# A decoder trunk's recurrence in another order: the first turned blocks later, the solve at the end of its own group, the masks ahead of the sample's steps, and the group norm centred by one product

## The chip, the cores and the metric

The kernel runs on one core of one Trainium2 chip. The metric is the device time of one execution in microseconds. The kernel before took 1679.8 us (median of 3 runs, 1679.66 to 1681.52).

## The reference

Two layers of a hybrid decoder act on a prompt of 256 tokens and on eight single sample tokens (264 columns in all, model width 1024). Each layer is a SwiGLU block, a mixer and a second SwiGLU block. The mixer's RWKV-7 group has 16 heads of 64; for each token it does

```
Sa = einsum('bhij,bhj->bhi', S, -kk_t)
S = S * w_t[:, :, None, :] + Sa[..., None] * b_t[:, :, None, :] + v_t[..., None] * k_t[:, :, None, :]
y_t = einsum('bhij,bhj->bhi', S, r_t)
...
mean = jnp.mean(y, axis=-1, keepdims=True)
var = jnp.mean(jnp.square(y - mean), axis=-1, keepdims=True)
y = ((y - mean) * lax.rsqrt(var + RWKV_GN_EPS)).reshape(Bsz, L, RWKV_DIM)
y = y * ln_w.astype(f32) + ln_b.astype(f32)
```

A short convolution group and a Mamba-2 group stand beside it; the three outputs are concatenated and multiplied by `w_out`.

## The kernel before

Each layer has a front stage (projections) and a back stage (`back_stage`), and only the back stage is touched. The five engines have one instruction list each, written out by hand. They meet by semaphores, and each list is done strictly in order, so the order of the calls is the schedule.

The 16 heads are worked as 8 pairs (`RT = 8`), one pair on 128 partitions. The prompt's recurrence is done in chunks of 64 tokens (`C = 64`, `NCH = 4`). Within a chunk the triangular system is inverted by doubling, in five levels (`LV = 5`), and several pairs are in the works at once. Loop turn `g` starts pair `g`, continues pair `b = g - 1`, does the states and outputs of pair `c = g - 2`, and the group norm of pair `p = g - 3`; `g` runs from 0 to 9. What the steps are, by their names:

- TensorE: `turn` transposes tokens, `gram(g+1)` makes the products of the next pair, `turn_x` puts the start of the inverse into PSUM, `level_t1(p, i)` and `level_u(p, i)` are the two products of a level (16 small matmuls each), `gv` and `solve` make u and w, `transfer`, `own_outputs`, `own_states` and `chunk` carry the state over the chunks, `turn_final` turns the last state, `mean_of` and `variance_of` sum over the 64 channels of each head, and `short(n)` are 24 large matmuls of the output projection with the two other groups' part (in turns 8 and 9, where pairs run out).
- ACT copies results from PSUM: `t1_copy` between the two products of a level, `x_copy` after a level, `tokens`, `rv_copy`, `uw_copy`, `state_copy`, `y_copy`, `variance`, and it squares (`square`). In turn 8 it also computes the inverse roots of five pairs' variances (`Ln`, then `Exp`, each with a load of its table), and it makes the high halves of weights (`ws.split_hi`).
- DVE: `mask` (two per pair, L2026), `start` (adds the identity, L2032), `turn_blocks` (L2038), `finish` (L2042), `transfer` (L2049, L2051), the eight steps `step(b, 0..7)` of the sample tokens (L2063 to L2081), `centre` (L2086), `gated` (L2092), scalings, and `ws.split_lo`.
- POOL: the first level (L1772), `level(p, i)` (the masked products of a level, two buffers, L1750), `weigh(g+1)` (four instructions, L1744), `key_row(b)` (L1758), `short_split_lo` (L1764), `ws.split_lo` (L216).

For pair `b` a level goes: `level` (POOL), `level_t1` (PE), `t1_copy` (ACT), `level_u` (PE, which also needs the blocks turned by DVE's `turn_blocks`), `x_copy` (ACT). `order_of` numbers the levels over all pairs, and `copied` the copies. PSUM bank `WB` is shared in turn by `gv`, `solve`, `mean_of` and `variance_of`. A new pair begins with `gram`, two masks, POOL's first level, `start`, and `turn_x`.

## Time and profile before

| | |
|---|---|
| median of 3 runs | 1679.8 us |
| the profiled execution | 1676.1 us, its span 1674.1 us |
| TensorE busy | 1550.2 us, 93% |
| VectorE busy | 1108.9 us, 66% |
| ScalarE busy | 881.6 us, 53% |
| GpSimd busy | 271.7 us, 16% |
| TensorE's mean granted clock | 0.978 |

The span goes from the first to the last instruction of one profiled execution. Times in rows are microseconds from its start. A timeline row has the start, the duration, the engine, the line, the operation, output and inputs with their shapes, the count of merged instructions, and in brackets the idle time before it with what ended it. TensorE's matmuls overlap, so the distance between two starts tells what a block of them takes to issue, and the duration how long until its last result is there. The back stages lie at about 440 to 605 us (layer 0) and 1266 to 1430 us (layer 1). The granted clock is 1.0 for TensorE's upper level of 2.4 GHz and 0.5 for the lower of 1.2 GHz.

### The profile page before, as it was taken

Reading aid. Unit: us, or ns where it says so; the run is one execution under the profiler, and the core shown is the slowest. Engines: PE = TensorE matmul, PEld = TensorE weight load, DVE = VectorE, ACT = ScalarE, POOL = GpSimd, SP = SyncE. Lnnn points to the kernel's source line nnn. Section 1 sums busy time; section 2 is a strip of 40 time slices with the busy share of each in tenths; the row PEclk is TensorE's granted clock in tenths of the full one; section 3 lists DMA queues with packets and bytes.
Section 4 is the critical chain, followed back from the end, with each engine's and each line's share of the span. In section 5 each row is a group of like instructions: output and inputs, shape, how many; then the busy total and the mean of one; then the engine's idle time right before and its main releaser. Section 6 shows DMA issues by size and latency. Waiting matters only on the chain. (4 is left out here: it accounts for less than half of the span.)

```text
span 1674.1 us, 39220 instructions
## 1 busy us (share of the span) xinstructions
PE 1550.2 (93%) x16355; PEld 1463.3 (87%) x16355; DVE 1108.9 (66%) x1758; ACT 881.6 (53%) x1579; POOL 271.7 (16%) x259
## 2 busy tenths in 40 slices
PE   7999999999688889999999999999996898899997
PEld 6999999987577789999999999989775777899997
DVE  5565587785577757665475655968765777576654
ACT  5444464767355655444353444647673456554443
POOL 0000003001265621000000000030013665300000
PEclk9999999999889999999999999999997999999999
DMA  7555556371134545655454655643702446355552
GB/s 229 178 177 165 168 170 203 112 209 50 50 106 130 156 135 176 193 162 188 163 185 151 202 165 177 192 151 117 224 1 72 122 132 183 118 185 193 178 181 71
DMA packets 280642, 256.15 MB, mean 153 GB/s; under 512 B 48054, under 2 KB 268700, under 8 KB 280450
## 3 DMA queue, kind: packets, MB, share of 16 engines
q1 hardware_dynamic: 276698, 252.05, 48.7%
q8 instruction: 131, 2.15, 0.6%
q10 hardware_dynamic: 3768, 1.59, 0.4%
q14 instruction: 45, 0.37, 0.1%
HBM read 242.22 MB, written 11.38 MB: 151 GB/s over the span
## 5 line engine op out<-in xcount | busy, mean ns | idle before, releaser
L209 ACT ACTIVATE front_hi<-front_raw 128x1024 fp32r<-128x1024 f32 (+2 forms) x230 | 238.5, 1039 | 260.7 <-PE ps L234 249.5
L216 DVE TENSOR_TENSOR front_lo<-front_raw,front_hi 128x1024 fp32r<-128x1024 f32 (+1 forms) x210 | 252.3, 1201 | 109.4 <-ACT front_hi L209 108.4
L209 ACT ACTIVATE out_hi<-out_raw 128x1024 fp32r<-128x1024 f32 (+1 forms) x168 | 173.2, 1038 | 215.6 <-PE ps L234 201.3
L216 DVE TENSOR_TENSOR out_lo<-out_raw,out_hi 128x1024 fp32r<-128x1024 f32 (+1 forms) x148 | 179.7, 1214 | 106.2 <-ACT out_hi L209 105.4
L232 PE MATMUL ps<-front_h_hi,front_hi 128*128 128x264 f32 (+1 forms) x816 | 240.8, 295 | 4.9 <-DVE front_lo L216 3.3
L234 PE MATMUL ps<-front_h_hi,front_lo 128*128 128x264 f32 (+1 forms) x816 | 232.4, 285 | 0.0
L233 PE MATMUL ps<-front_h_lo,front_hi 128*128 128x264 f32 (+1 forms) x816 | 232.3, 285 | 0.0
L232 PE MATMUL ps<-ffn_h_hi,out_hi 128*128 128x264 f32 x704 | 200.4, 285 | 0.1
L233 PE MATMUL ps<-ffn_h_lo,out_hi 128*128 128x264 f32 x704 | 199.6, 284 | 0.0
L234 PE MATMUL ps<-ffn_h_hi,out_lo 128*128 128x264 f32 x704 | 199.6, 283 | 0.0
L232 PE MATMUL ps<-in_h_hi,front_hi 128*128 128x264 f32 x688 | 196.5, 286 | 0.0
L233 PE MATMUL ps<-in_h_lo,front_hi 128*128 128x264 f32 x688 | 195.6, 284 | 0.0
L234 PE MATMUL ps<-in_h_hi,front_lo 128*128 128x264 f32 x688 | 195.6, 284 | 0.0
L232 PEld LDWEIGHTS ps<-front_h_hi,front_hi 128*128 128x128 f32 (+1 forms) x816 | 153.7, 188 | 13.6 <-issue 11.9
L233 PEld LDWEIGHTS ps<-front_h_lo,front_hi 128*128 128x128 f32 (+1 forms) x816 | 153.7, 188 | 0.7
L234 PEld LDWEIGHTS ps<-front_h_hi,front_lo 128*128 128x128 f32 (+1 forms) x816 | 153.0, 188 | 0.1
L216 POOL TENSOR_TENSOR front_lo<-front_raw,front_hi 128x1024 fp32r<-128x1024 f32 (+1 forms) x20 | 49.8, 2490 | 543.0 <-ACT front_hi L209 543.0
L232 PEld LDWEIGHTS ps<-ffn_h_hi,out_hi 128*128 128x128 f32 x704 | 132.4, 188 | 0.6 <-ACT ffn_h_hi L283 0.5
L233 PEld LDWEIGHTS ps<-ffn_h_lo,out_hi 128*128 128x128 f32 x704 | 132.4, 188 | 0.1
L234 PEld LDWEIGHTS ps<-ffn_h_hi,out_lo 128*128 128x128 f32 x704 | 132.3, 188 | 0.0
L233 PEld LDWEIGHTS ps<-in_h_lo,front_hi 128*128 128x128 f32 x688 | 130.4, 190 | 0.1
L232 PEld LDWEIGHTS ps<-in_h_hi,front_hi 128*128 128x128 f32 x688 | 130.3, 189 | 0.1
(400 smaller groups left out, 3826.2 us busy)
## 6 DMA issues: line engine op xcount, KB each, us to landing
front_raw<-in_w_in SPq DMA_DIRECT2D x50, 1024.0 KB, 5.3
out_raw<-in_ffn_w_in SPq DMA_DIRECT2D x44, 1024.0 KB, 5.2
front_raw<-in_ffn_w_in SPq DMA_DIRECT2D x40, 1024.0 KB, 5.3
back_sample_rows<-row_scratch SPq DMA_DIRECT2D x160, 128.0 KB, 3.1
out_raw<-in_w_out SPq DMA_DIRECT2D x16, 1024.0 KB, 5.2
front_raw<-in_ffn_w_out SPq DMA_DIRECT2D x16, 896.0 KB, 4.7
out_raw<-in_ffn_w_out SPq DMA_DIRECT2D x16, 896.0 KB, 4.7
front_raw<-in_ffn_w_out SPq DMA_DIRECT2D x8, 1024.0 KB, 5.0
```

The lines of the kernel that those rows point to most:

```text
L209: act.activation(self.hi[n % self.RING][:, 0:k, 0:w], self._raw(n), ACT.Copy).then_inc(self.hi_ready, 1)
L216: eng.tensor_tensor(self.lo[n % self.RING][:, 0:k, 0:w], self._raw(n), self.hi[n % self.RING][:, 0:k, 0:w].bitcast(F32), ALU.subtract).the ...
L232: pe.matmul(out, hi[:, j, 0:w], x_hi[:, j], start=start and j == 0, stop=False)
L233: pe.matmul(out, hi[:, j, 0:w], x_lo[:, j], start=False, stop=False)
L234: mm = pe.matmul(out, lo[:, j, 0:w], x_hi[:, j], start=False, stop=stop and j == k - 1)
```

## The change

Nothing of the recurrence's arithmetic is added or left out; most of the diff moves calls.

- **TensorE.** `solve` moves from the head of the next turn (`solve(c)`) to the end of its own (`solve(b)`). The token transposes `turn(g, 0)` and `turn(g, 1)` go together ahead of `level_u(b, 2)`, and `turn_x(g)` behind it. The order of levels becomes (b, 2), (b, 3), (g, 0), (b, 4), (g, 1), where it was (b, 2), (g, 0), (b, 3), (g, 1), (b, 4). `variance_of(p)` goes behind `gram(g+1)`. In turn 8 `short(0)` stands between `level_t1(7, 2)` and `level_u(7, 2)`; in turn 9 `short(2)` stands behind `transfer(7)`.
- **DVE.** `turn_blocks(b, 2)` moves from the end of the group that made them (`turn_blocks(g, 2)`) to the head of the next. The masks of the next pair are ahead of steps 4 and 5. `transfer(c)` is ahead of `turn_blocks(b, 3)`. The scalings of `ys` are spread over four turns, two in each.
- **POOL.** `weigh(g+1)` is ahead of `level(g, 0)`, `level(b, 2)` is at the head of the next turn (in turn 8 behind `short_split_lo` and `ws.split_lo`).
- **ACT.** Follows TensorE's order; `decays` run one pair further ahead; `variance(p)` is directly ahead of `t1_copy(b, 4)`.
- **Group norm.** A new constant `centre` is the identity less 1/64 in each head's block. `mean_of` multiplies by it and so gives the deviation itself, in PSUM. DVE's `centre` goes; `square` and `gated` read PSUM, `gated` waits for `square`, and `variance_of`, which writes the same bank, waits for `gated`.

```diff
+    parts["centre"] = np.eye(P) - same / HS
...
-            order = [(g - 1, 2), (g, 0), (g - 1, 3), (g, 1), (g - 1, 4)]
+            order = [(g - 1, 2), (g - 1, 3), (g, 0), (g - 1, 4), (g, 1)]
...
-            for pair, i in [(g, 0), (g - 1, 3), (g, 1), (g - 1, 4), (g, 2)]:
+            for pair, i in [(g - 1, 3), (g, 0), (g - 1, 4), (g, 1), (g, 2)]:
```

GpSimd's list:

```diff
-                        level(g, 0)
                     if b >= 0:
+                        level(b, 2)
                         level(b, 3)
                     if g + 1 < RT:
                         weigh(g + 1)
                     if g < RT:
-                        level(g, 1)
-                    if g == RT - 1:
-                        for q in range(3):
-                            short_split_lo(q)
+                        level(g, 0)
                     if b >= 0:
                         level(b, 4)
                     if g == RT:
                         ws.split_lo(pool, 2)
+                    if g < RT:
+                        level(g, 1)
                     if b >= 0:
                         key_row(b)
                     if g == RT - 1:
-                        short_split_lo(3)
-                    if g < RT:
-                        level(g, 2)
-                    if g == RT - 1:
+                        for q in range(4):
+                            short_split_lo(q)
                         ws.split_lo(pool, 0)
```

The group norm:

```diff
-                    act.wait_ge(s("dev_done"), p + 1)
+                    act.wait_ge(s("mean_ps"), p + 1)
...
-                    act.activation(v[:, p], dev[:, p], ACT.Square).then_inc(s("dev_sq"), 1)
+                    act.activation(v[:, p], ps[:, WB, 0:N], ACT.Square).then_inc(s("dev_sq"), 1)
...
-                def centre(p):
-                    dve.wait_ge(s("mean_ps"), p + 1)
-                    dve.scalar_tensor_tensor(out=dev[:, p], in0=ps[:, WB, 0:N], scalar=-1.0 / HS, in1=r[:, p],
-                                             op0=ALU.mult, op1=ALU.add).then_inc(s("dev_done"), 1)
...
-                    dve.wait_ge(s("dev_done"), p + 1)
+                    dve.wait_ge(s("dev_sq"), p + 1)
...
-                    pe.matmul(ps[:, WB, 0:N], head, r[:, p], start=True, stop=True).then_inc(s("mean_ps"), 1)
+                    pe.matmul(ps[:, WB, 0:N], centre, r[:, p], start=True, stop=True).then_inc(s("mean_ps"), 1)
...
+                    pe.wait_ge(s("dev_gated"), p + 1)
```

TensorE's turn after the change, as its calls follow (conditions left out):

```
level_t1(b, 2); turn_final(c - 1); turn(g, 0); turn(g, 1); short(0) in turn 8; level_u(b, 2); turn_x(g)
transfer(c); short(2) in turn 9; level_t1(b, 3); mean_of(p); level_u(b, 3); level_t1(g, 0); short(3) in turn 9
own_outputs(c); own_states(c); level_u(g, 0); level_t1(b, 4); chunk(c, 1); short(1) in turn 8; gram(g + 1)
variance_of(p); level_u(b, 4); level_t1(g, 1); chunk(c, 2); gv(b); level_u(g, 1); chunk(c, 3); solve(b)
```

ACT's turn after the change:

```
uw_copy(c); t1_copy(b, 2); split_hi(4), split_hi(5) in turn 9; final_copy(c - 1); tokens(g, 0); tokens(g, 1)
x_copy(b, 3); x_copy(g, 0); Ln, Exp, split_hi(2) in turn 8; t1_copy(b, 3); square(p); x_copy(b, 4)
t1_copy(g, 0); state_copy(c, 0); x_copy(g, 1); decays(g + 2); variance(p); t1_copy(b, 4); state_copy(c, 1)
split_hi(3) in turn 8; t1_copy(g, 1); rv_copy(b); state_copy(c, 2); x_copy(g, 2); state_copy(c, 3); y_copy(c)
split_hi(0), split_hi(1) in turn 7; two y copies in turn 8
```

## Rows read from the trace of the kernel before

**Rows 1.** The page, busy time, share and instructions of each engine.
```profile
PE 1550.2 (93%) x16355; PEld 1463.3 (87%) x16355; DVE 1108.9 (66%) x1758; ACT 881.6 (53%) x1579; POOL 271.7 (16%) x259
```
**Rows 2.** Waits, 440 to 600 us: us in total, times, longest.
```profile
PE ps L2230 <- DVE back_inverse_t L2032: 10.8, 8, 3.6
PE ps L2275 <- DVE back_inverse_t L2042: 5.5, 5, 3.8
```
**Rows 3.** Timeline of TensorE in the middle of layer 0's back stage.
```profile
523.94 0.68 PE L2230 MATMUL ps<-cst,back_inverse_t 64*64 64x64 f32 x16 [1.03 <-DVE back_inverse_t L2032]
...
536.57 1.09 PE L2275 MATMUL ps<-back_gv_a,back_inverse_t 64*64 64x128 f32 x16 [0.29 <-DVE back_inverse_t L2042]
...
538.91 0.68 PE L2230 MATMUL ps<-cst,back_inverse_t 64*64 64x64 f32 x16 [1.02 <-DVE back_inverse_t L2032]
539.43 0.63 PE L2218 MATMUL ps<-back_n_x,back_inverse_t 64*64 64x64 f32 x16
```
**Rows 4.** Timeline of TensorE: `turn_x(1)`, and `level_u` of pairs 0 and 6, both layers.
```profile
458.12 1.12 PE L2230 MATMUL ps<-cst,back_inverse_t 64*64 64x64 f32 x16 [3.61 <-DVE back_inverse_t L2032]
459.02 1.06 PE L2218 MATMUL ps<-back_n_x,back_inverse_t 64*64 64x64 f32 x16
...
554.99 0.63 PE L2218 MATMUL ps<-back_n_x,back_inverse_t 64*64 64x64 f32 x16
...
1285.13 1.06 PE L2218 MATMUL ps<-back_n_x,back_inverse_t 64*64 64x64 f32 x16
...
1378.80 0.63 PE L2218 MATMUL ps<-back_n_x,back_inverse_t 64*64 64x64 f32 x16
```
**Rows 5.** Timeline of ACT: the copy of a variance in a middle group.
```profile
532.06 0.39 ACT L1873 ACTIVATE xs<-ps 128x264 f32<-128x264 f32 x1 [0.30 <-PE ps L2355]
```
**Rows 6.** Timeline of DVE in two middle groups.
```profile
532.34 0.95 DVE L2092 SCALAR_TENSOR_TENSOR gate<-xs,cols,gate 128x264 f32<-128x264 f32 x1
...
534.29 1.29 DVE L2026 TENSOR_TENSOR back_products<-ps,cst 128x512 f32<-128x512 f32 x2
...
544.67 0.42 DVE L2086 SCALAR_TENSOR_TENSOR xs<-ps,xs 128x264 f32<-128x264 f32 x1
```
**Rows 7.** Timeline of POOL in turn 7 of layer 0.
```profile
559.88 4.73 POOL L1764 TENSOR_TENSOR short_lo<-y_short,short_hi 128x528 fp32r<-128x528 f32 x3 [2.18 <-ACT short_hi L1863]
...
569.98 2.58 POOL L216 TENSOR_TENSOR out_lo<-out_raw,out_hi 128x1024 fp32r<-128x1024 f32 x1 [1.11 <-ACT out_hi L209]
```
**Rows 8.** Timeline of ACT in turns 8 and 9 of layer 0.
```profile
572.88 0.39 ACT L1829 ACTIVATE back_inverse<-ps 128x256 f32<-128x256 f32 x1 [1.14 <-PE ps L2218]
...
579.45 0.36 ACT L1822 ACTIVATE back_n_x<-ps 128x256 f32<-128x256 f32 x1
...
591.04 1.99 ACT L209 ACTIVATE out_hi<-out_raw 128x1024 fp32r<-128x1024 f32 x2
```
**Rows 9.** Timeline of TensorE in turns 8 and 9 of layer 0, `mean_of(6)` also of layer 1.
```profile
572.17 0.68 PE L2218 MATMUL ps<-back_n_x,back_inverse_t 64*64 64x64 f32 x15 [0.73 <-issue]
...
575.90 0.46 PE L2296 MATMUL ps<-back_tok,back_u_w 64*64 64x64 f32 x16
...
579.87 0.62 PE L2218 MATMUL ps<-back_n_x,back_inverse_t 64*64 64x64 f32 x13 [1.56 <-ACT back_n_x L1822]
...
593.34 0.46 PE L2296 MATMUL ps<-back_tok,back_u_w 64*64 64x64 f32 x16 [1.79 <-ACT back_final_state L1854]
...
593.97 0.71 PE L2351 MATMUL ps<-xs,cst 128*128 128x264 f32 x2
...
1417.51 0.71 PE L2351 MATMUL ps<-xs,cst 128*128 128x264 f32 x2
```
**Rows 10.** Windows: stretch, length, busy time of engines, granted clock, DMA share, GB/s.
```profile
458.00:463.00 5.00, 4.88 (x72) 4.44 (x74) 1.08 (x3) 2.25 (x6) 2.43 (x4) 0.50 0.03 3
...
842.00:846.00 4.00, 2.85 (x13) 2.88 (x14) 1.23 (x1) 2.87 (x3) 0.75 (x5) 0.59 0.41 116
```
**Rows 11.** Timeline of TensorE between the layers.
```profile
843.15 0.56 PE L232 MATMUL ps<-in_h_hi,first_hi 128*128 128x264 f32 x1 [3.39 <-PEq L143]
```

More of the change, by code:

```diff
@@ L1907, in _ @@
                         decays(1)
+                    if c >= 0:
+                        uw_copy(c)
                     if 0 <= b < RT:
@@ L1929, in _ @@
                         ws.split_hi(act, 2)
+                    if 0 <= b < RT:
+                        t1_copy(b, 3)
+                    if p >= 0:
+                        square(p)
+                    if 0 <= b < RT:
+                        x_copy(b, 4)
+                    if g == RT - 1:
+                        short_split_hi(0)
+                        short_split_hi(1)
                     if g < RT:
@@ L1940, in _ @@
                         shift_store(3 * g)
-                        if g == 1:
-                            shift_rows(4)
-                    if g == RT - 1:
-                        short_split_hi(0)
-                        short_split_hi(1)
-                    if 0 <= b < RT:
-                        t1_copy(b, 3)
-                    if g < RT:
-                        tokens(g, 1)
-                    if p >= 0:
-                        square(p)
-                    if 0 <= b < RT:
-                        x_copy(b, 4)
+                    if g + 2 < RT:
+                        decays(g + 2)
+                    if p >= 0:
+                        variance(p)
+                    if 0 <= b < RT:
+                        t1_copy(b, 4)
+                    if c >= 0:
+                        state_copy(c, 1)
+                    if g == 1:
+                        shift_rows(5)
+                        shift_store(4)
                     if g == RT - 1:
@@ L2113, in _ @@
                     if 0 <= b < RT:
+                        step(b, 0)
+                    if c >= 0:
+                        transfer(c)
+                    if 0 <= b < RT:
                         turn_blocks(b, 3)
-                        step(b, 0)
+                        step(b, 1)
                     if g == RT + 1:
                         ws.split_lo(dve, 3)
-                    if c >= 0:
-                        transfer(c)
+                    if p >= 0:
+                        gated(p)
+                    if 0 <= b < RT:
+                        turn_blocks(b, 4)
+                        step(b, 2)
                     if g < RT:
@@ L2122, in _ @@
                     if 0 <= b < RT:
-                        step(b, 1)
-                    if p >= 0:
-                        centre(p)
+                        step(b, 3)
+                    if g + 1 < RT:
+                        mask(g + 1, 0)
+                        mask(g + 1, 1)
                     if 0 <= b < RT:
-                        step(b, 2)
-                        turn_blocks(b, 4)
-                        step(b, 3)
-                    if p >= 0:
-                        gated(p)
-                    if g < RT:
-                        turn_blocks(g, 2)
+                        step(b, 4)
+                        step(b, 5)
+                        finish(b)
                     if g < 4:
@@ L2162, in _ @@
                 y_split_lo(1)
-                centre(RT - 1)
                 gated(RT - 1)
@@ L2394, in _ @@
                         shift_turn(4)
-                    if c >= 0:
-                        solve(c)
                     if c >= 1:
                         turn_final(c - 1)
-                    if g == RT + 1:
-                        short(2)
-                    if g < RT:
-                        turn_x(g)
+                    if g and g < RT:
+                        turn(g, 0)
+                        turn(g, 1)
+                    if g == RT:
+                        short(0)
                     if 0 <= b < RT:
@@ L2405, in _ @@
                     if g < RT:
-                        level_t1(g, 0)
-                        turn(g, 0)
-                    if g == RT:
-                        short(0)
+                        turn_x(g)
                     if c >= 0:
                         transfer(c)
+                    if g == RT + 1:
+                        short(2)
+                    if 0 <= b < RT:
+                        level_t1(b, 3)
                     if p >= 0:
                         mean_of(p)
+                    if 0 <= b < RT:
+                        level_u(b, 3)
                     if g < RT:
-                        level_u(g, 0)
-                    if 0 <= b < RT:
-                        level_t1(b, 3)
-                    if g < RT:
-                        turn(g, 1)
+                        level_t1(g, 0)
+                    if g == 0:
+                        turn(0, 0)
+                        turn(0, 1)
                     if g == RT + 1:
@@ L2432, in _ @@
                         shift_turn(6)
-                    if p >= 0:
-                        variance_of(p)
-                    if g == RT:
-                        short(1)
                     if g < RT:
-                        level_u(g, 1)
+                        level_u(g, 0)
                     if 0 <= b < RT:
@@ L2442, in _ @@
                         chunk(c, 1)
+                    if g == RT:
+                        short(1)
                     if g + 1 < RT:
                         gram(g + 1)
+                    if p >= 0:
+                        variance_of(p)
                     if 0 <= b < RT:
-                        gv(b)
+                        level_u(b, 4)
+                    if g < RT:
+                        level_t1(g, 1)
                     if g == RT + 1:
```

66 lines of the change are left out of this document (26 added, 40 removed).

## The prediction

> **What bounds the kernel now.** I read the page first, then the waits of one back stage, then its timeline engine by engine. TensorE is busy for 1550.2 of 1674.1 us [rows 1], so only its idle time and its slow stretches can be won. The change touches the back stage alone (about 440 to 605 us in layer 0, 1266 to 1430 in layer 1). There the waits name two places: `turn_x` waits 10.8 us in eight groups for the identity added by DVE (L2032), and `solve` 5.5 us for `finish` (L2042) [rows 2]. In an undisturbed group the timeline shows both: 0.29 us before `solve`, 1.03 us before `turn_x` [rows 3]; from one `turn_x` to the next are 523.94 to 538.91, 14.97 us. The first two groups are longer, because TensorE stands still for 3.6 us before `turn_x(1)` (458.12) and then runs at the half clock (0.50, the 1.2 GHz level): the same sixteen products of `turn_x` are issued in 0.90 us there against 0.51 at full clock (459.02 less 458.12; 539.43 less 538.91) [rows 3, 4].
>
> **Part 1, the middle groups (gain).** I rebuilt a group from the start-to-start distances of the timeline. 14.97 less the two idles is 13.65 us [rows 3]. The new order puts `turn_x` after two transposes and a product, so the chain masks (1.29 for both, L2026), POOL's first level, DVE's start has over 5 us from the end of `gram(g+1)`, and no longer decides. It adds these waits:
> - ACT now has the copy of the variance (0.39) ahead of `t1_copy(b,4)`, and TensorE has `variance_of` directly ahead of `level_u(b,4)`. A product of this size ends 0.71 us after it began, its copy takes 0.39 (the next copy can start 0.33 behind it, an estimate from the neighbouring starts), and a copy of four blocks 0.38: with 0.05 and 0.08 for the two hand-overs that is 1.55 us, while TensorE is free again after about 0.65. So about 0.9 us idle in each group from g = 3 [rows 5, 8, 9].
> - DVE's two instructions of `transfer(c)` now stand ahead of `turn_blocks(b,3)`; each is a 0.42 us instruction on PSUM [rows 6], and `level_u(b,3)` waits about 0.15 for the turned block.
>
> Sum 14.7 us. Groups 2 and 3 also carry two bonus and two `ys` scalings (four of about 0.4, as a PSUM instruction of that size takes [rows 6]) ahead of steps 6 and 7: I take 14.8 for both. If the 0.9 does not arise it is 13.8, if DVE (with POOL beside it) falls behind, 15.7; I take 14.7, since it comes from durations of the same instructions.
>
> **Part 2, the first groups (gain).** In group 0 POOL does the four instructions of `weigh(1)` before `level(0,0)`, which delays `level_t1(0,0)`, but `gram(1)` still waits for `tokens(0,1)` and stays at its place. `level_u(0,2)` now stands ahead of `turn_x(1)` and needs no `start(1)`; it comes by my count 0.4 us earlier than its 459.02. From there to `level_u(1,2)` the same count (part 1's group without norm, states and outputs, DVE's scalings included) gives 13.2 us at full clock, and 14.5 with 1.3 us for one slow stretch, because by my estimate TensorE still has pauses of over 1 us in group 0. I take 14.5, with 13.2 and about 17 (two slow stretches) as the ends. Sum from `level_u(0,2)` to `level_u(6,2)`: 14.5 + 14.8 + 14.8 + 3 x 14.7 = 88.2 us. Before, it was 554.99 - 459.02 = 95.97 in layer 0 and 1378.80 - 1285.13 = 93.67 in layer 1 [rows 4]. **Gain 7.8 and 5.5 us**, and the 0.4 in each layer: 14.1 us together.
>
> **Part 3, the last two groups (loss).** Here the new order puts things in a row that ran side by side. I count from `level_u(6,2)` = 0, in both layers. By part 1's group, less `gram` (there is no pair 8) and with ACT's four `short_split_hi` put in, `y_copy(5)` ends at 11.9 and TensorE has issued `solve(6)` at 12.7.
> - `level(7,2)` on POOL stood ahead of `ws.split_lo(0)`; now it stands behind four `short_split_lo` (three take 4.73) and behind this split (2.58) [rows 7]. The split waits for ACT's `split_hi(0)`, half of 1.99 us, after `y_copy(5)` [rows 8]: 12.8, POOL's split ends 15.4, level 16.3, `level_t1(7,2)` 16.5: **3.8 us idle**.
> - `short(0)`, 24 products, about 3.1 us (572.17 to 575.90 less one block), is now ahead of `level_u(7,2)`. ACT copies x (0.38), then runs Ln and Exp with two table loads and `split_hi(2)`, before `t1_copy(7,3)`. This run is 572.88 to 579.45 on ACT and 572.17 to 579.87 on TensorE [rows 8, 9]. Before, it covered `short(0)`; now it begins after it, at 20.3, and `level_u(7,3)` comes at 28.0. TensorE has 2.3 us of other work: **5.4 us idle**.
> - To the end of `solve(7)`: `own_outputs`, which was ahead, adds 0.5, and the variance wait of part 1 comes again (0.9), then `split_hi(3)` between ACT's two copies 0.9: 38.2.
> - `short(2)` no longer stands between `solve(7)` and `transfer(7)`. The latter waits for ACT's two y copies, `uw_copy`, two splits (1.99) and `final_copy` [rows 8]: 42.3, **3.8 us idle**. Then 0.63 and `short(2)` 3.1: 46.0.
>
> Before, this state (`mean_of(6)` begins) came at 593.97 - 554.99 = 38.98 and 1417.51 - 1378.80 = 38.71 [rows 9]. **Loss 7.0 and 7.3 us.** Bounds: 4 us per layer if POOL and ACT come early, 9 if they are held up by DVE's contention.
>
> **Part 4, the group norm (small gain).** `centre` on DVE (0.42, L2086) goes; TensorE's product keeps its size with another constant [rows 6]. In the middle groups DVE is not last. At the end ACT squares 0.45 us earlier, and the chain to `short(6)` shortens by that: 0.9 us in all. The gated product now reads PSUM: beside POOL its old form with two SBUF operands takes 0.95, while the PSUM form L2086 took 0.42 in the middle of POOL's work [rows 6]. The Trainium skill, page "Advanced Engine Details and Errata", section "GPSIMD Details", says that POOL's interface conflicts with DVE instructions that have two SBUF inputs; the trace agrees, and this would save another half microsecond of DVE time, which is hidden. One more constant (64 KB) is loaded at the start: 0 to 0.3 us, taken as 0.
>
> **Part 5, the clock (loss).** After every idle of over 3 us that I looked at, the granted clock falls: 458 to 463 at 0.50 after 3.61 us, 842 to 846 at 0.59 after 3.39 us [rows 4, 10, 11]. What it costs: of the 4.88 us busy in 458 to 463 half, 2.4 us; at 843.15, where 2.9 us of the slow stretch were left, 1.5. Part 3 makes three such idles in each layer, each with dense work behind it. At 2.0 each, 6 x 2.0 = 12 us (9 to 20). By the Trainium skill, page "TensorE: Matmul & The Clock Gate", section "Why this matters for your kernels", such idles between bursts are to be avoided, since the clock then falls back to half; the rule speaks against this change exactly where part 3 places the idles, while the long idles of the first groups go.
>
> **Sum.** -14.1 + 14.3 - 0.9 + 12 = +11.3 us on the profiled execution's 1676.1 us (its span 1674.1 and 2.0 around it), so 1687.4. The median of the runs (1679.8) lies 3.7 above that execution, and the forecast is for the median: 1679.8 + 11.3 = 1691.1.
>
> **The rivals.**
> - *A, the clock holds (0.17).* The idles of part 3 arise but no slow stretch follows, as after the 1.79 us before `transfer(7)`, whose 32 products then take 0.63 us to issue, full pace [rows 9]. Then -0.7 us: 1679.1. Against it: my idles are twice as long.
> - *B, faster (0.22).* The variance wait does not arise, since square and copy find ACT free earlier, and the middle groups run at 13.8 us: 5 x 0.9 x 2 = 9 us less, on top of A: 1670. It decides if TensorE's idle before `level_u(b,4)` is under 0.2 us. For it: both copies are short. Against: the wait is one of order, not of load. With the clock falling, this case is 1682.
> - *C, DVE or POOL bounds the groups (0.11).* Period 15.7 because instructions with two SBUF operands meet POOL (0.95 for L2092) [rows 6]. 10 x 1.0 us more: 1701.
> - *D, nothing moves (0.03).* The masks were not what held `turn_x`; 1680. Against: the waits name the identity's line.
> - *Forecast (0.47).* 1691.1; with its own bounds (clock 9 to 20, part 3 by 2 per layer) 1684 to 1701.
>
> **How the numbers follow.** Cases of both signs hold much of the chance, so the range goes from B to just over C: 1670 to 1702. A measurement of this kernel tells 0.2% (3.4 us) from no change. Faster by more: B, most of it, and a little of A: 0.22. Within: the rest of A, of B with the slow clock, and D: 0.19. Slower: forecast and C: 0.59.
>
> **What would show it.** After the change: distance between two `level_u(b,2)` of groups 4 to 6 (14.7); idle before `level_u(b,4)` caused by `t1_copy` (0.9); no wait of `turn_x` for L2032; in the last groups idles of about 3.8, 5.4 and 3.8 us before `level_t1(7,2)`, `level_u(7,3)` and `transfer(7)`; granted clock 0.5 behind each. If these idles are under 2 us, or the clock stays at 1.0 behind them, the forecast is wrong and A or B holds. If the period is over 15.2, C holds.

## The result and the profile after

| | before | after |
|---|---|---|
| median of the runs, side by side | 1679.7 us | 1710.8 us |
| the profiled execution | 1676.1 us | 1708.6 us |
| its span | 1674.1 us | 1706.5 us |
| TensorE's mean granted clock | 0.978 | 0.964 |

The change makes the kernel slower: the ratio of after to before is 1.0188, with a 95% interval of 1.0155 to 1.0221. The forecast was 1691.1 us in a range of 1670 to 1702. Its sign was right, but it forecast 11.3 us of loss where 31.1 came, and the time lies outside the range.

Page of after, busy time of the engines. It answers [rows 1]: the same number of products keeps TensorE busy for 5 us more, at a lower mean clock, and the span is 32 us longer. The other 27 us are idle time.
```profile
PE 1555.5 (91%) x16355; PEld 1474.8 (86%) x16355; DVE 1105.7 (65%) x1742; ACT 877.6 (51%) x1579; POOL 279.0 (16%) x259
```
Waits of TensorE in the groups of layer 0 (467 to 562 us): what waits, for whom, us in total, times, longest. It answers [rows 2]: `turn_x` no longer waits for the identity (L2032), and `solve` little for `finish` (L2042), as the forecast said. In their place `level_u` waits for the turned blocks (L2038) and for the copies of t1 (L1820).
```profile
PE ps L2210 <- DVE back_inverse_t L2038: 7.4, 3, 2.8
PE ps L2210 <- ACT back_n_x L1820: 4.3, 7, 0.8
PE ps L2267 <- DVE back_inverse_t L2042: 1.5, 2, 0.8
```
The same view of the last two groups (560 to 625 us): three long waits, 4.84 us ahead of `level_t1(7,2)`, 5.17 ahead of `level_u(7,3)` and 3.60 ahead of `transfer(7)`.
```profile
PE ps L2210 <- ACT back_n_x L1820: 7.1, 4, 5.2
PE ps L2210 <- POOL back_n_levels L1751: 4.8, 1, 4.8
PE ps L2288 <- ACT back_final_state L1852: 3.6, 1, 3.6
```
At the same three places before waits for 0.60, 1.56 and 1.79 us; the last two are in [rows 9], and this is the first, from the timeline of TensorE in before:
```profile
568.92 0.68 PE L2218 MATMUL ps<-back_inverse,back_n_levels 64*64 64x64 f32 x16 [0.60 <-POOL back_n_levels L1750]
```
Timeline of TensorE in after, answering [rows 3, 4, 9]. The first rows are `level_u(0,2)`, `level_u(b,2)` of group 3, `level_u` of level 4 in two groups, and at 555.82 `level_u(6,2)`; from 578.01 on they are `level_t1(7,2)`, `level_u(7,3)`, `transfer(7)` and `mean_of(6)`, in layer 0 and then in layer 1, which begins with `level_u(6,2)`.
```profile
462.55 0.68 PE L2210 MATMUL ps<-back_n_x,back_inverse_t 64*64 64x64 f32 x16
...
494.47 0.68 PE L2210 MATMUL ps<-back_n_x,back_inverse_t 64*64 64x64 f32 x16 [2.68 <-DVE back_inverse_t L2038]
...
521.29 0.68 PE L2210 MATMUL ps<-back_inverse_t,back_n_x 64*64 64x64 f32 x16 [0.76 <-ACT back_n_x L1820]
...
536.09 0.68 PE L2210 MATMUL ps<-back_inverse_t,back_n_x 64*64 64x64 f32 x16 [0.76 <-ACT back_n_x L1820]
...
555.82 0.68 PE L2210 MATMUL ps<-back_n_x,back_inverse_t 64*64 64x64 f32 x16
...
578.01 1.12 PE L2210 MATMUL ps<-back_inverse,back_n_levels 64*64 64x64 f32 x16 [4.84 <-POOL back_n_levels L1751]
...
590.80 1.00 PE L2210 MATMUL ps<-back_n_x,back_inverse_t 64*64 64x64 f32 x13 [5.17 <-ACT back_n_x L1820]
...
606.43 0.70 PE L2288 MATMUL ps<-back_tok,back_u_w 64*64 64x64 f32 x16 [3.60 <-ACT back_final_state L1852]
...
612.45 0.61 PE L2343 MATMUL ps<-xs,cst 128*128 128x264 f32 x2
...
1395.33 0.68 PE L2210 MATMUL ps<-back_n_x,back_inverse_t 64*64 64x64 f32 x16
...
1414.22 1.12 PE L2210 MATMUL ps<-back_inverse,back_n_levels 64*64 64x64 f32 x16 [4.83 <-POOL back_n_levels L1751]
...
1427.03 1.01 PE L2210 MATMUL ps<-back_n_x,back_inverse_t 64*64 64x64 f32 x13 [5.17 <-ACT back_n_x L1820]
...
1448.67 0.61 PE L2343 MATMUL ps<-xs,cst 128*128 128x264 f32 x2
```
To see where the 32 us lie, I divided each profiled execution at three blocks of TensorE: the start of `turn_x(0)`, of `turn_x(7)` and of `mean_of(7)` in each layer. The kernels e1 to e12 are those of the experiments below. "Groups" is the stretch from the first to the second, "last groups" from the second to the third. All in us:

| kernel | up to turn_x(0) | groups, layer 0 | last groups, layer 0 | between | groups, layer 1 | last groups, layer 1 | rest |
|---|---|---|---|---|---|---|---|
| before | 445.7 | 108.7 | 49.4 | 667.5 | 107.0 | 49.1 | 246.8 |
| after | 449.1 | 107.2 | 66.2 | 667.0 | 106.3 | 62.9 | 247.7 |
| e1 | 446.5 | 108.4 | 55.8 | 665.6 | 107.1 | 52.5 | 246.7 |
| e2 | 448.9 | 107.7 | 62.5 | 665.5 | 104.1 | 59.3 | 248.0 |
| e3 | 446.8 | 109.2 | 60.9 | 665.6 | 106.0 | 57.0 | 249.2 |
| e4 | 446.0 | 111.3 | 65.4 | 665.5 | 106.0 | 61.2 | 246.5 |
| e8 | 446.7 | 107.0 | 63.9 | 667.0 | 109.5 | 59.8 | 247.7 |
| e9 | 445.9 | 112.2 | 67.1 | 666.1 | 104.7 | 61.9 | 247.0 |
| e6 | 446.6 | 105.1 | 55.8 | 665.3 | 102.1 | 53.7 | 246.6 |
| e7 | 446.0 | 107.7 | 55.3 | 665.6 | 104.7 | 52.3 | 246.2 |
| e10 | 449.0 | 101.9 | 52.6 | 665.5 | 102.0 | 49.5 | 248.3 |
| e11 | 446.6 | 105.0 | 51.4 | 665.7 | 100.4 | 49.7 | 246.7 |
| e5 | 446.9 | 112.6 | 54.0 | 667.1 | 113.7 | 55.9 | 249.2 |
| e12 | 446.0 | 110.2 | 52.9 | 665.6 | 106.2 | 50.2 | 246.4 |

The last groups lose 16.8 and 13.8 us, 30.6 together. TensorE was busy for 41.7 and 41.8 us of them in before and for 46.2 and 44.2 in after, so 6.9 us of the loss are products that take longer (the mean clock of the two stretches is 0.82 and 0.84, and was 1.00), and 23.7 are idle time. The seven groups ahead of them gain 1.5 and 0.7. The columns outside of the recurrence show how far one execution strays from another: no edit touches the stretch up to `turn_x(0)` in e1 to e4 and e8, and it takes 446.0 to 448.9 us there and 449.1 in after. In these six kernels (after, e1 to e4, e8) the groups before `turn_x(7)` are the same code but for GpSimd's level 2 of pair 7 at the very end, and they take 107.0 to 111.3 us in layer 0 (mean 108.5) and 104.1 to 109.5 in layer 1 (mean 106.5). So a column is good to some 2 us, and the reordering alone gave nothing there that can be told from before's 108.7 and 107.0.

### The profile page after: what moved, and what is told of

Same layout as the page of the kernel before. It is cut to its first block and busy times, and to the rows that moved or that the text cites. A ratio compares the mean times of both kernels' runs of the same rounds, so it can differ in the third digit from the quotient of the medians.

```text
span 1706.5 us, 39204 instructions
## 1 busy us (share of the span) xinstructions
PE 1555.5 (91%) x16355; PEld 1474.8 (86%) x16355; DVE 1105.7 (65%) x1742; ACT 877.6 (51%) x1579; POOL 279.0 (16%) x259
```

## The experiments

**Theory T1:** what loses is the order of the last groups. **T2:** VectorE's scalings hold groups 2 to 4. **T3:** the wait for the variance's copy costs its 0.76 us in each group. **T4:** the clock that falls behind each idle costs about 2 us. The norm was forecast to be worth 0.9 us. Every ratio below is to the kernel before, with its 95% interval.

### e1, the order of the last groups undone

```diff
 # GpSimd, group 7; level(b, 2) skipped in group 8
                     if g == RT - 1:
+                        level(g, 2)
                         for q in range(4):
                             short_split_lo(q)
 # TensorE, group 8
-                    if g == RT:
-                        short(0)
                     if 0 <= b < RT:
                         level_u(b, 2)
+                    if g == RT:
+                        short(0)
 # TensorE, group 9
+                    if g == RT + 1:
+                        short(2)
                     if c >= 0:
                         transfer(c)
-                    if g == RT + 1:
-                        short(2)
```


> The changed kernel with the three pieces of its last groups put back as they stood before: GpSimd multiplies level 2 of pair 7 in group 7, ahead of the four short_lo subtractions, and not in group 8 behind split_lo(0); TensorE runs short(0) behind level_u(7,2) and not ahead of it; short(2) runs ahead of transfer(7) and fills its wait. Theory T1 (the tail order makes the loss): the waits of 4.84 us (POOL) and 3.60 us (final state) go or are filled and short(0) no longer delays the chain by its 2.6 us, in both layers: 2 x (4.3 + 2.6 + 2.6) = 19 us, and with the half-clock stretches behind those waits up to 28; time 1683 to 1692 us, ratio to before 1.002 to 1.007. Rival T2 (the groups in the middle make the loss, the tail's idle would be met again elsewhere): less than 6 us gained, 1705 to 1711.

Measured: 1684.2 us, ratio 1.0040 (1.0024 to 1.0055). Of after's 1.0188 the three moves alone take back 0.0148, about 25 us. T1 holds, and its number too. The last groups shorten by 10.4 us in each layer. They still take 6.4 and 3.4 us more than before. One wait shows which part is left, 3.27 us in layer 0 and 4.59 in layer 1. Timeline of TensorE in e1, `level_u(7,2)`:
```profile
575.71 1.12 PE L2212 MATMUL ps<-back_n_x,back_inverse_t 64*64 64x64 f32 x16 [3.27 <-DVE back_inverse_t L2040]
```
and of VectorE ahead of it: the turning of pair 7's blocks stands behind the low half of the output weights, and this one had waited 4.22 us for ACT.
```profile
572.68 2.53 DVE L217 TENSOR_TENSOR out_lo<-out_raw,out_hi 128x1024 fp32r<-128x1024 f32 x1 [4.22 <-ACT out_hi L210]
575.13 0.43 DVE L2040 STREAM_TRANSPOSE back_inverse_t<-back_inverse 128x256 f32<-128x256 f32 x1
```
e10 moves it.

### e2, GpSimd's level alone

```diff
                     if b >= 0:
-                        level(b, 2)
+                        if g < RT:
+                            level(b, 2)
                         level(b, 3)
...
                     if g == RT - 1:
+                        level(g, 2)
                         for q in range(4):
                             short_split_lo(q)
```


> The changed kernel with only GpSimd's level 2 of pair 7 put back into group 7, right behind key_row and ahead of the short_lo subtractions. T1: the wait of 4.84 us at level_t1(7,2) falls under 1 us in both layers, 8 us and at most 4 of clock besides: 1698 to 1703 us. Rival: the chain waits at the next place (ACT's queue with Ln, Exp and split_hi(2) ahead of t1_copy(7,3)), because that queue is set by what ACT began earlier and not by level 2: under 3 us gained, 1708 to 1711.

Measured: 1703.0 us, ratio 1.0152 (1.0137 to 1.0167), 0.0036 or 6 us less than after; the last groups are 3.7 and 3.6 us shorter. The end of the forecast interval is just met, but not the 8 us: TensorE comes to `short(0)` earlier and waits there 2.57 us for GpSimd's split of the output weights. So more than half of the wait only changed its place. What GpSimd did in after (timeline, layer 0): `level(7,2)` is the first of the three at 576.25, behind the last two `short_lo` subtractions, which waited 3.60 us for ACT, and the split of the weights.
```profile
568.83 3.01 POOL L1765 TENSOR_TENSOR short_lo<-y_short,short_hi 128x528 fp32r<-128x528 f32 x2 [3.60 <-ACT short_hi L1861]
573.94 2.35 POOL L217 TENSOR_TENSOR out_lo<-out_raw,out_hi 128x1024 fp32r<-128x1024 f32 x1 [2.10 <-ACT out_hi L210]
576.25 3.71 POOL L1751 TENSOR_TENSOR back_n_levels<-back_products,cst 128x256 f32<-128x256 f32 x3
```

### e3, short(0) alone

```diff
-                    if g == RT:
-                        short(0)
                     if 0 <= b < RT:
                         level_u(b, 2)
+                    if g == RT:
+                        short(0)
```


> The changed kernel with only short(0) put back behind level_u(7,2). e1 took 25 us off the changed kernel and e2 (level 2 of pair 7 alone) 6; this run and the next divide the other 19. Theory T1 (each piece is on the chain by its own): short(0) is 24 products, 2.6 to 3.5 us, ahead of level_u(7,2), and behind it the same products would fill TensorE's wait for ACT's t1_copy(7,3): 5 to 10 us less in the two layers, 1701 to 1706 us. Rival (the wait for level 2 of pair 7 is not removed here, and what short(0) gives up is lost in the next wait): under 3 us, 1708 to 1712.

Measured: 1694.3 us, ratio 1.0094 (1.0080 to 1.0109): 0.0094 or 16 us less than after, more than either expectation. The last groups are 5.3 and 5.9 us shorter, 11 of the 16; this is the largest of the three pieces. The mechanism is ACT's long block. Timeline of ACT in after: the copy of x for level 3 of pair 7, then the table load that begins Ln and Exp, then `split_hi(2)`, and only then the copy of t1 on which `level_u(7,3)` waits.
```profile
583.83 0.38 ACT L1827 ACTIVATE back_inverse<-ps 128x256 f32<-128x256 f32 x1 [4.04 <-PE ps L2210]
584.23 1.28 ACT L1928 ACT_TABLE_LOAD   x1
...
589.44 1.04 ACT L210 ACTIVATE out_hi<-out_raw 128x1024 fp32r<-128x1024 f32 x1
590.39 0.36 ACT L1820 ACTIVATE back_n_x<-ps 128x256 f32<-128x256 f32 x1
```
From 583.83 to 590.39 are 6.56 us in which the chain can't go on, and for 5.17 us of it TensorE has nothing else to do. In e3 `short(0)` runs in that time. The wait at `level_u(7,3)` is 0.26 us where it was 5.17, although ACT's block is as long as it was (580.63 to 587.20). Timelines of ACT and of TensorE in e3:
```profile
580.63 0.38 ACT L1827 ACTIVATE back_inverse<-ps 128x256 f32<-128x256 f32 x1 [0.98 <-PE ps L2210]
...
587.20 0.36 ACT L1820 ACTIVATE back_n_x<-ps 128x256 f32<-128x256 f32 x1
```
```profile
587.62 0.62 PE L2210 MATMUL ps<-back_n_x,back_inverse_t 64*64 64x64 f32 x13 [0.26 <-ACT back_n_x L1820]
```

### e4, short(2) alone

```diff
+                    if g == RT + 1:
+                        short(2)
                     if c >= 0:
                         transfer(c)
-                    if g == RT + 1:
-                        short(2)
```


> The changed kernel with only short(2) put back ahead of transfer(7), into its wait of 3.60 us for ACT's copies. T1: short(2) is 24 products, 3.0 us at full clock, that now stand behind transfer(7) and ahead of the own outputs: 2 x 3 = 6 us less, up to 10 with the clock kept: 1701 to 1705 us. Rival (short(2) meets its halves late and waits by itself there): under 3 us, 1708 to 1711.

Measured: 1700.7 us, ratio 1.0126 (1.0111 to 1.0142), 0.0062 or 10 us less than after by the medians. In its profile the last groups are only 0.8 and 1.7 us shorter: the wait ahead of `transfer(7)` shrinks from 3.60 to 0.54, and 1.45 of it comes back right behind, as a wait of `short(3)` for VectorE's `out_lo`. The remainder of the 10 us lies in columns that the edit does not touch; one execution does not settle it.

In the last groups the three pieces alone sum to 9.8 and 11.2 us, and together, in e1, they give 10.4 and 10.4. By the medians they sum to 0.0192 against 0.0148. e4's median lies just below its first expectation, but in its profile the last groups show only a quarter of the gain.

### e8, the same waits without idle

```diff
+                def fill(bank, count):
+                    for _ in range(count):
+                        pe.transpose(ps[:, bank, 0:P], ident, ident)
...
+                    if g == RT:
+                        pe.wait_ge(s("tok_in"), 3 * RT)
+                        fill(GB, 20)
                     if 0 <= b < RT:
                         level_t1(b, 2)
```
and in the same way 24 ahead of `level_u(7,3)` and 16 ahead of `transfer(7)`.

> The changed kernel with transposes of the identity into PSUM banks that nobody reads at that time, put on TensorE into the three largest waits of the tail of each layer: 20 ahead of level_t1(7,2) (wait of 4.84 us), 24 ahead of level_u(7,3) (5.17 us), 16 ahead of transfer(7) (3.60 us); at 0.15 us each at full clock they take 3.0, 3.6 and 2.4 us. The chain of dependences is the same, only TensorE does not idle. Theory T4 (the clock's fall behind an idle costs about 2.0 us, the forecast's part 5): six of them kept away, 8 to 12 us less: 1699 to 1703 us, and the half-clock stretches behind these waits are gone from the profile. Rival (the clock costs little, since at half clock TensorE still ends before the engines it waits for): 1709 to 1712 us though the stretches are gone.

Measured: 1702.5 us, ratio 1.0148 (1.0131 to 1.0164). A kernel with 120 more products is 0.0040, or 7 us, faster than the changed kernel. The two intervals overlap by 0.0009; taken together they leave 0.0037 on either side of the 0.0040, so the gain is just clear of nothing. The transposes took less time than expected, 0.12 us each, so they fill only about half of the waits. Timeline of TensorE in e8: the first filling, and the idle that is left.
```profile
570.63 2.40 PE L2379 MATMUL ps<-cst 128*128 128x128 f32 x20
575.56 0.68 PE L2210 MATMUL ps<-back_inverse,back_n_levels 64*64 64x64 f32 x16 [2.53 <-POOL back_n_levels L1751]
```
Windows of after: stretch, length, busy time of the engines, granted clock, DMA share, GB/s. Behind the idles of 5.17 us and 3.60 us the clock was at its lower level for most of each window:
```profile
587.00:595.00 8.00, 4.20 (x105) 4.12 (x106) 3.04 (x5) 4.72 (x7) 3.82 (x2) 0.57 0.01 2
604.00:612.00 8.00, 5.57 (x53) 5.49 (x54) 1.89 (x3) 2.28 (x4) 2.36 (x1) 0.57 0.33 107
```
The same windows of e8, where idles of 2.55 and 1.86 us are left: after the first the clock still falls, for a shorter time, and after the second it does not.
```profile
587.00:595.00 8.00, 6.44 (x126) 6.32 (x127) 4.83 (x6) 2.49 (x6) 3.82 (x2) 0.79 0.01 2
601.00:609.00 8.00, 6.14 (x76) 5.80 (x75) 2.24 (x4) 3.18 (x6) 2.35 (x1) 1.00 0.41 132
```
The last groups are 2.3 and 3.1 us shorter, 5.4 for the six places, 0.9 each. Four of the six places still have a slow stretch, so the clock's whole cost there should be larger; but each column is good to some 2 us only, so 0.9 is an estimate and no bound. T4 holds in kind; its 2.0 each is not reached.

### e9, the new order with the old group norm

```diff
-                    dve.wait_ge(s("dev_sq"), p + 1)
+                    dve.wait_ge(s("dev_done"), p + 1)
...
                     if p >= 0:
-                        gated(p)
+                        centre(p)
...
                         step(b, 3)
+                    if p >= 0:
+                        gated(p)
...
-                    pe.matmul(ps[:, WB, 0:N], centre, r[:, p], start=True, stop=True)
+                    pe.matmul(ps[:, WB, 0:N], head, r[:, p], start=True, stop=True)
```


> The changed kernel with the old group norm (product with head, centre on VectorE in the place where gated stands, gated behind step 3, square from the centred rows). e5 showed the new norm 21.3 us slower in the old order. If the norm costs of itself, this one is 5 to 20 us faster than the changed kernel (1690 to 1705). If it cost in the old order alone, because gated stood too late on VectorE, this one is slower than the changed kernel by the centring's 0.42 us ahead of the square in some ten groups and by the later copy: 1711 to 1718.

Measured: 1705.6 us, ratio 1.0155 (1.0139 to 1.0172). Against after's 1.0188 (1.0155 to 1.0221) that is 0.0033 less, with about 0.0037 on either side: in the new order the new norm costs between nothing and 0.7%. The profiled spans are 1705.0 and 1706.5. Neither expectation is met clearly, so whether the norm costs here stays open; the bulk of the loss comes with the order alone.

### e5 and e12, the new group norm in the old order

e5 is before with the norm's edit alone. e12 moves one more call; the diff shows VectorE's list of e12 against before:
```diff
                     if 0 <= b < RT:
                         step(b, 1)
                     if p >= 0:
-                        centre(p)
+                        gated(p)
                     if 0 <= b < RT:
                         step(b, 2)
                         turn_blocks(b, 4)
                         step(b, 3)
-                    if p >= 0:
-                        gated(p)
```


> The kernel before with the group norm's change alone: mean_of multiplies by eye minus head/64, ACT squares and VectorE gates out of PSUM, centre is gone, variance_of also waits for gated. The forecast's part 4: 0.9 us less at the end of the second layer, nothing elsewhere: 1678 to 1680 us, ratio 0.999 to 1.000. Rival: variance_of waits for gated, which stands on VectorE behind turn_blocks(b,4) and step 3, so the chain of every group is held by 0.3 to 1 us in ten groups: 1683 to 1690 us.

> e5 (the group norm's change alone, in the old order) with VectorE's gated moved from behind step 3 to behind step 1, where centre stood. In e5 variance_of waits 1.05 us in each group for gated, which stands behind turn_blocks(b,4) and the 1.14 us of step 3, and the groups take 16.6 us and not 15.0. If that place is the whole of e5's loss of 21.3 us, this kernel takes 1677 to 1682 us, ratio 0.999 to 1.001, and the groups are back at 15.0 us. Rival (the new norm costs in any order, as a product and a gate that read PSUM behind each other): 1688 to 1697.

Measured: e5 1699.5 us, ratio 1.0126 (1.0110 to 1.0143); e12 1678.0 us, ratio 1.0000 (0.9990 to 1.0009). The 0.9 us of the forecast can't be told from nothing, and a misplaced gate costs 21 us. e5 lies above both of its expectations: the rival named the right place and made it too cheap. e12 met its first one. Timeline of TensorE in e5: from one `turn_x` to the next are 526.24 to 542.84, 16.60 us against 14.97 in before [rows 3], with a new wait of 1.05 us ahead of `variance_of`.
```profile
526.24 0.68 PE L2222 MATMUL ps<-cst,back_inverse_t 64*64 64x64 f32 x16 [1.03 <-DVE back_inverse_t L2033]
...
535.26 0.69 PE L2348 MATMUL ps<-xs,cst 128*128 128x264 f32 x2 [1.05 <-DVE gate L2088]
...
542.84 0.68 PE L2222 MATMUL ps<-cst,back_inverse_t 64*64 64x64 f32 x16 [1.03 <-DVE back_inverse_t L2033]
```
Timeline of VectorE in e5: `gated` (L2088) is short, since it reads PSUM (0.48 where [rows 6] has 0.95), but it stands behind `turn_blocks(b,4)` and step 3.
```profile
533.20 0.45 DVE L2039 STREAM_TRANSPOSE back_inverse_t<-back_inverse 128x256 f32<-128x256 f32 x1
533.57 1.14 DVE L2072 TENSOR_TENSOR back_outer<-back_sample_rows,back_sample_sa 128x512 f32<-128x512 f32 x1
534.63 0.48 DVE L2088 SCALAR_TENSOR_TENSOR gate<-ps,cols,gate 128x264 f32<-128x264 f32 x1
```
In e12 the product at L2348 follows without a wait. Its groups take 15.78 us in layer 0 and 14.97 in layer 1 (1336.03 to 1351.00 between two `turn_x`). In the old norm nothing on TensorE waited for `gated`; in the new one the bank of the centred rows is freed by it, so it has come onto the chain, and its place decides. The changed kernel has it in the early place already.

### e6, the scalings spread

e1, and:
```diff
-                    if g < 4:
-                        for m in (2 * g, 2 * g + 1):
+                    if g < RT:
+                        for m in (g,):
...
-                    for i in range(2 * g, 2 * g + 2) if g < ST else ():
+                    for i in (range(2) if g == 0 else range(g + 1, g + 2) if g < 7 else ()):
```


> e1 (the tail put back) with VectorE's scalings spread: one bonus product and about one y_short product in each group instead of two and two in groups 0 to 3 (bonus(m) in group m, y_short 0 and 1 in group 0, then one a group to group 6). Theory T2: in groups 2 to 4 TensorE waits 2.0 to 2.8 us for turn_blocks(b,2), which stands behind 3.2 us of scalings and step 6; half of them gone takes 1.6 us off each of three groups in both layers, 8 us or more with the clock: 1674 to 1678 us, ratio 0.996 to 0.999 to the kernel before. Rival: the middle groups, where VectorE waited for nothing of it, now pay 0.8 us in each of four groups: no gain, 1682 to 1687.

Measured: 1676.6 us, ratio 0.9982 (0.9970 to 0.9994), 0.0058 or 10 us less than e1. The groups are 3.3 and 5.0 us shorter. Timeline of VectorE in after, ahead of the wait of 2.68 us at 494.47: four scalings take 3.09 us (489.00 to 492.09), and step 6 1.16.
```profile
489.00 1.49 DVE L2136 SCALAR_TENSOR_TENSOR bonus<-bonus,cols,gate 128x264 f32<-128x264 f32 x2
490.42 1.75 DVE L2141 SCALAR_TENSOR_TENSOR y_short<-y_short,cols,ssm_root 128x264 f32<-128x264 f32 x2
492.09 1.16 DVE L2079 TENSOR_TENSOR back_prod<-back_sample_wkv,back_sample_rows 128x512 f32<-128x512 f32 x1
...
493.89 0.43 DVE L2038 STREAM_TRANSPOSE back_inverse_t<-back_inverse 128x256 f32<-128x256 f32 x1
```
In e6 two of the four are left there, 1.42 us (487.53 to 488.95), and TensorE's wait at that place is 1.02 us:
```profile
487.53 0.62 DVE L2138 SCALAR_TENSOR_TENSOR bonus<-bonus,cols,gate 128x264 f32<-128x264 f32 x1
488.08 0.95 DVE L2143 SCALAR_TENSOR_TENSOR y_short<-y_short,cols,sc_root 128x264 f32<-128x264 f32 x1
```
```profile
491.34 0.68 PE L2212 MATMUL ps<-back_n_x,back_inverse_t 64*64 64x64 f32 x16 [1.02 <-DVE back_inverse_t L2040]
```
T2 holds: the wait is 1.66 us shorter, and 3.09 - 1.42 = 1.67 us left the queue.

### e7, the variance later

e1, and:
```diff
 # ACT
-                    if p >= 0:
-                        variance(p)
                     if 0 <= b < RT:
                         t1_copy(b, 4)
+                    if p >= 0:
+                        variance(p)
 # TensorE
-                    if p >= 0:
-                        variance_of(p)
                     if 0 <= b < RT:
                         level_u(b, 4)
+                    if p >= 0:
+                        variance_of(p)
```


> e1 with variance_of moved behind level_u(b,4) on TensorE and the variance's copy behind t1_copy(b,4) on ACT. In five groups a layer level_u(b,4) waits 0.76 us for t1_copy(b,4), which stands behind that copy. Theory T3: the wait goes, 0.5 to 0.76 us in each of about 12 groups: 1675 to 1679 us. Rival: gv(b), which needs the copy to have freed the bank, waits in its place: 1682 to 1686.

Measured: 1680.9 us, ratio 1.0015 (1.0005 to 1.0025), 0.0025 or 4 us less than e1. The waits of 0.76 us are gone (the longest wait of TensorE for L1822, the copy of t1, is 0.6 us in the groups), and 4 of the 0.76 x 12 = 9 us came. The result lies between the two expectations. T3 holds in place; less than half of the wait was worth time. Part of it came back: the wait for the turned blocks in group 4 of layer 0 is 2.49 us, where e1 has 2.01.

### e10 and e11, what the waits point to

e10 is e1 with e6's and e7's edits and
```diff
-                    if g == RT - 1:
-                        ws.split_lo(dve, 1)
...
                     if 0 <= b < RT:
                         turn_blocks(b, 2)
+                    if g == RT:
+                        ws.split_lo(dve, 1)
```
e11 also has VectorE's `split_lo(3)` at the end of group 8 instead of behind `transfer(7)`.

> e1 with both edits, scalings spread and the variance later, and with VectorE's split_lo(1) moved from the end of group 7 behind turn_blocks(7,2): in e1 level_u(7,2) waits 3.27 us for turn_blocks(7,2), which stands behind that split (it waits for ACT's split_hi(1)). If the three waits are independent: 8 + 7 + 5 us off e1, 1663 to 1669 us, ratio 0.990 to 0.994. Rival (the chain's other waits take their place): not below 1675.

> e10 with VectorE's split_lo(3) moved from group 9, behind transfer(7), to the end of group 8, ahead of normed(0). In e10 short(3) waits 1.46 us for it in each layer. If the wait is on the chain: 2 to 3 us less than e10, 1669 us, ratio 0.994. Rival: the wait at the next split takes its place, ratio as e10's 0.9957 within 0.0008.

Measured: e10 1671.8 us, ratio 0.9957 (0.9944 to 0.9969); e11 1669.0 us, ratio 0.9939 (0.9925 to 0.9952). Both beat both kernels; e11 is 10 us faster than before and 42 faster than the change. e10 did not reach its 0.990 to 0.994: in layer 0 the wait at `level_u(7,2)` went from 3.27 to 1.80 us and is now one for ACT. e11's step is worth 3 us by the medians, as expected, but the two intervals overlap by 0.0008. Page of e11, to be held against [rows 1]: TensorE is busy for 9 us less at the same number of products, which fits its mean granted clock of 0.981 against 0.978.
```profile
PE 1541.3 (93%) x16355; PEld 1459.5 (88%) x16355; DVE 1107.7 (67%) x1742; ACT 879.4 (53%) x1579; POOL 280.6 (17%) x259
```

## Why the prediction missed

**Part 1 and 2, the groups: wrong, the costliest step.** The forecast took 14.1 us of gain up to `level_u(6,2)`. Over the executions of the same order there is none that can be told from zero; in after itself `level_u(6,2)` is 2.5 us earlier in layer 0 and 1.6 in layer 1, counted from `turn_x(0)`. By the forecast's own marks, `level_u(0,2)` to `level_u(6,2)`, after takes 93.27 us in layer 0 (462.55 to 555.82) and 90.01 in layer 1 (1305.32 to 1395.33), where 88.2 was counted. What the part said of the mechanism holds: `turn_x` is free, and the last groups before `turn_x(7)` take 14.8 and 14.4 us in layer 0 and 13.9 in layer 1 against 14.97 before. The step that failed is the sentence on groups 2 and 3, "four of about 0.4" and 14.8 us for each. VectorE took 0.75 and 0.88 for each scaling, 3.1 us for the four where I had 1.6. The price fits these very instructions, both operands in SBUF, in the place that they had before: 0.43 us each, while GpSimd is idle. Timelines of VectorE and of GpSimd in before:
```profile
468.09 0.86 DVE L2136 SCALAR_TENSOR_TENSOR bonus<-bonus,cols,gate 128x264 f32<-128x264 f32 x2
...
469.27 1.70 DVE L2141 SCALAR_TENSOR_TENSOR y_short<-y_short,cols,ssm_root 128x264 f32<-128x264 f32 x4
```
```profile
472.85 1.10 POOL L1772 TENSOR_TENSOR back_inverse_t<-back_products,cst 128x256 f32<-128x256 f32 x1 [4.85 <-DVE back_products L2026]
```
The change put them beside GpSimd's work. Timeline of GpSimd in after, at the four scalings of 489.00 to 492.09:
```profile
488.16 2.04 POOL L1751 TENSOR_TENSOR back_n_levels<-back_products,cst 128x256 f32<-128x256 f32 x2
490.17 0.87 POOL L1745 TENSOR_TENSOR back_b_k<-minus_b,back_decays 128x256 f32<-128x256 f32 x1
```
What the forecast left out is this neighbour. The row of 0.42 that it took [rows 6] was no bound for it, since that instruction has an operand in PSUM, and L2092 in the same group of rows, with both in SBUF and GpSimd at work, has 0.95. Besides, I gave them 0.1 us a group, as if they lay beside other work; but they stand ahead of steps 6 and 7 and of `turn_blocks(b,2)`, which is now the first link of the next group. From `turn_x(2)` to `turn_x(3)` and on to `turn_x(4)` were 16.8 and 17.1 us in layer 0, 16.8 and 16.1 in layer 1, together 7.6 us more than four times 14.8. e6 shows this: with half of them moved the groups gain 3.3 and 5.0 us. The Trainium skill, page "Advanced Engine Details and Errata", section "GPSIMD Details", says that GpSimd's interface conflicts with VectorE instructions with two SBUF inputs; the traces agree (beside GpSimd 0.48 for e5's gate out of PSUM, 0.75 and 0.88 for these), and I used the rule only for what it saved and not for what it cost.

**The variance wait: right.** 0.9 forecast, 0.76 measured. e7 puts its value at 4 us in all. Rival B, which lived of its absence, falls.

**Part 3, the order of the last groups: right in kind, too short.** Forecast idles 3.8, 5.4 and 3.8 us; measured 4.84, 5.17 and 3.60, ahead of the instructions that were named and for the releasers that were named. e1 shows that this order makes 25 of the 31 us of the loss, and e3 that ACT's block without cover is its largest piece. Forecast from `level_u(6,2)` to `mean_of(6)` without the clock: 46.0. Measured: 612.45 - 555.82 = 56.63 in layer 0 and 1448.67 - 1395.33 = 53.34 in layer 1. So there are 10.6 and 7.3 us beyond the count, where part 5 had 6 and 6. Against before the loss is 17.6 and 14.6 us. `level_t1(7,2)` alone came 5.7 and 2.4 us later than the 16.5 counted (578.01 - 555.82 and 1414.22 - 1395.33). Of this 1.0 is the longer idle in each layer, and 2.85 in layer 0 a wait at which nothing in the profile is late; before has a like one of 2.4. The rest of it stays open.

**Part 5, the clock: right in kind, and rather too large.** The clock fell behind each of the six idles, as forecast. e8, which fills each of them by about half, took 7 us off. A second estimate comes from the count of part 3: from `level_t1(7,2)` to `level_u(7,3)`, on to `transfer(7)` (606.43 and 1442.67) and on to `mean_of(6)` TensorE took 1.3, 1.3 and 2.3 us more than counted, in both layers alike. That is 9.9 us where 12 stood, if the count is right in all else. The Trainium skill, page "TensorE: Matmul & The Clock Gate", section "Why this matters for your kernels", says that idles between bursts are to be avoided; e8 agrees with its 7 us. Rival A (the clock holds) falls. What was missed is that shorter idles can do it as well, and not each time: behind the 2.68 us in group 3 the window 492 to 500 of after has 0.79, behind the same 2.68 us in layer 1 (window 1335 to 1343) it has 1.00, behind 2.01 us at 511.60 (window 509 to 517) 0.79 again. The forecast gave the groups no slow stretch there. That it comes and goes in the same code is part of the spread of the columns.

**Part 4, the norm: right that it is small.** e12 gives 1.0000 with 0.0009 on either side, so the 0.9 us (0.0005) can't be told. Not seen was how much hangs on the place of `gated`.

**Rivals C and D.** C (VectorE with GpSimd bounds the groups) had the right mechanism, and part of the place: not in all groups, but in the three (2 to 4) that come behind scalings. Its time of 1701 was the nearest. D falls.

In sum: -14.1 became about -1 to -4 (4.2 in after's own profile), +14.3 and +12 became +32.2 by the same marks (17.6 and 14.6), and -0.9 became nothing. The range was too narrow since its upper end put C's cost in place of the forecast's gain but never beside a longer tail.

## What to carry to other kernels

Take the price of a moved instruction from a row with the same operands in the same memories and with the neighbour at work that it will have in its new place; its own old row is not enough (0.43 us there, 0.75 to 0.88 here). A long block on one engine (here table loads, Ln, Exp and a split, 6.6 us on ACT) needs other work of TensorE placed behind the instruction that starts it and not ahead of it. When an instruction becomes the one that frees a buffer, look at what stands ahead of it in its queue: half a microsecond of gate cost 21 us behind step 3 and nothing that can be measured ahead of it.

## What the runs showed of the hardware

- A kernel that runs 120 useless transposes in its waits was 7 us faster (ratio 1.0148 against 1.0188) than the one that idles there (e8); less of the work behind them ran at the lower clock level (0.79 against 0.57, 1.00 against 0.57).
- The granted clock fell behind each of the six idles of 3.6 to 5.2 us in after. Behind idles of 2.0 to 2.8 us it fell at some places (0.79 in 492 to 500 us and in 509 to 517 us of after) and not at others (1.00 in 1335 to 1343 us); behind one of 1.86 us in e8 it did not (1.00 in 601 to 609 us).
- A `scalar_tensor_tensor` of 128 x 264 with both operands in SBUF took 0.43 us while GpSimd was idle (before, 468 to 471 us) and 0.62 to 0.95 while it worked; with one operand in PSUM it took 0.48 beside GpSimd too (e5).
